# Output projections by three single-pass products, the low parts of their weights on GpSimd

## The reference

```
for l in range(DEPTH):                      # 2
    h = rmsnorm(x, norm1_g[l])
    proj = h @ w_in[l]
    ya, yb, yc, yd = ...                    # pooling, attention, convolution, spatial gating
    br = jnp.einsum('bsic,icd->bsid', br, w_branch[l])
    gates = jax.nn.sigmoid(h @ w_gate[l] + b_gate[l]).reshape(B, S, N_BRANCH, D)
    merged = jnp.sum(gates * br, axis=2)
    x = x + merged @ w_out[l]
    h2 = rmsnorm(x, norm2_g[l])
    x = x + swiglu(h2, ...)                 # l = 0, dense
    x = x + moe_ffn(h2, ...)                # l = 1, top 2 of 8 experts
```

## Time and profile before

| | us |
|---|---|
| runs shown (3) | 1772.56, 1776.92, 1777.15; median 1776.92 |
| profiled execution | 1776.46 |
| its span | 1773.4 |
| PE busy | 1642.1 (93%) |
| DVE busy | 1327.5 (75%) |
| ACT busy | 1097.2 (62%) |
| POOL busy | 323.4 (18%) |

### The profile page before, as it was taken

One profiled execution on the slowest core, in us unless ns is written; L12 is line 12 of the kernel. 1 busy time (PEld: TensorE's weight loads), 2 busy tenths in 40 slices (PEclk: granted clock), 3 DMA queues, 4 the chain that ended last, 5 costly groups with the idle time before them and its releaser, 6 DMA issues.

```text
span 1773.4 us, 22987 instructions
## 1 busy us (share of the span) xinstructions
PE 1642.1 (93%) x9076; PEld 1411.0 (80%) x9076; DVE 1327.5 (75%) x1346; ACT 1097.2 (62%) x1236; POOL 323.4 (18%) x93
## 2 busy tenths in 40 slices
PE   2987998999897789779999999999999999999998
PEld 2977976999797788468888878878888888888786
DVE  2779454545467955368988998988898888989896
ACT  3572614333456362257777877877877877777775
POOL 6758530000365854020000000000000000000000
PEclk9988999999999899889999999999999999999999
DMA  7533435555544233869999999999999999999991
GB/s 184 178 121 104 132 119 181 180 186 190 179 131 143 87 127 119 296 237 363 354 368 340 360 352 334 375 348 341 375 345 349 366 341 352 365 341 355 364 362 44
DMA packets 231254, 460.55 MB, mean 260 GB/s; under 512 B 7418, under 2 KB 79334, under 8 KB 231142
## 3 DMA queue, kind: packets, MB, share of 16 engines
q1 hardware_dynamic: 229888, 456.68, 73.3%
q0 software_dynamic: 832, 1.74, 0.6%
q10 hardware_dynamic: 422, 0.61, 0.1%
HBM read 457.96 MB, written 1.05 MB: 259 GB/s over the span
## 4 chain that ended last, share of the span: by engine, by line
PE 80%; DVE 15%; ACT 2%; issue 1%; DVEq 0%; ACTq 0%
PE bank L905 17%; PE bank L906 17%; PE bank L909 17%; PE bank L690 6%; PE bank L692 6%; PE bank L691 6%; DVE arena L1440 3%; PE bank L735 3%; PE bank L933 2%; PE bank L940 2%; PE bank L969 1%; DVE shared8k L1583 1%; DVE shared8k L1455 1%; DVE qk_raw L1373 1%; ACT w_hi L496 1%
## 5 line engine op out<-in xcount | busy, mean ns | idle before, releaser
L547 DVE TENSOR_TENSOR w_lo<-arena,w_hi 128x1024 fp32r<-128x1024 f32 x486 | 579.2, 1220 | 81.4 <-ACT w_hi L541 69.5
L541 ACT ACTIVATE w_hi<-arena 128x1024 fp32r<-128x1024 f32 x492 | 517.4, 1061 | 146.9 <-PE bank L909 146.6
L504 POOL TENSOR_TENSOR w_lo<-ring,w_hi 128x2048 fp32r<-128x2048 f32 x56 | 293.9, 5254 | 377.5 <-ACT w_hi L496 377.5
L905 PE MATMUL bank<-w_hi,h_hi 128*128 128x512 f32 x896 | 358.5, 400 | 1.4 <-DVE h_lo L1657 1.4
L906 PE MATMUL bank<-w_hi,h_lo 128*128 128x512 f32 x896 | 349.1, 390 | 0.0
L690 PE MATMUL bank<-h_hi,w_hi 128*128 128x256 f32 x992 | 292.1, 294 | 27.3 <-POOL w_lo L504 22.1
L691 PE MATMUL bank<-h_lo,w_hi 128*128 128x256 f32 x992 | 288.0, 290 | 0.0
L692 PE MATMUL bank<-h_hi,w_lo 128*128 128x256 f32 x992 | 287.6, 290 | 0.0
L909 PE MATMUL bank<-w_lo,h_hi 128*128 128x512 f32 x896 | 276.4, 390 | 0.0
L547 DVE TENSOR_TENSOR w_lo<-ring,w_hi 128x1024 fp32r<-128x1024 f32 x180 | 215.0, 1220 | 27.0 <-ACT w_hi L541 23.0
L541 ACT ACTIVATE w_hi<-ring 128x1024 fp32r<-128x1024 f32 x180 | 189.8, 1062 | 54.3 <-PE bank L909 54.2
(11 more groups left out here) (235 smaller groups left out, 1920.3 us busy)
## 6 DMA issues: line engine op xcount, KB each, us to landing
arena<-in_moe_w SPq DMA_DIRECT2D x246, 1024.0 KB, 5.8
ring<-in_moe_w SPq DMA_DIRECT2D x90, 1024.0 KB, 5.8
ring<-in_ffn_w SPq DMA_DIRECT2D x33, 1024.0 KB, 5.3
ring<-in_w_gate SPq DMA_DIRECT2D x32, 1024.0 KB, 5.3
ring<-in_w_in SPq DMA_DIRECT2D x16, 1024.0 KB, 5.3
ring<-in_w_branch SPq DMA_DIRECT2D x8, 1024.0 KB, 4.8
ring<-in_w_out SPq DMA_DIRECT2D x8, 1024.0 KB, 4.8
x_tok<-in_x SPq DMA_DIRECT2D x2, 512.0 KB, 6.2
```

The source lines that it names most:

```text
L504: eng.tensor_tensor(w_lo[:, m % LO, :], raw, w_hi[:, m % HI, :].bitcast(F32), ALU.subtract)\
L541: nc.scalar.activation(half_hi[:, m % AHEAD, :], raw_of(n)[:, HALF * (m % 2):HALF * (m % 2) + HALF], ACT.Copy)\
L547: eng.tensor_tensor(half_lo[:, m % AHEAD, :], raw_of(m // 2)[:, HALF * (m % 2):HALF * (m % 2) + HALF], half_hi[:, m % AHEAD, :].bitcast(F3 ...
L905: pe.matmul(dst, hi, w[:, cols], start=first(x), stop=False)
```

## The change

The output projections leave the fp32 form. Each of their products is made by `three`, from high and low parts of `merged` and of the weights. Four things follow. The "out" units are in the list of splits, so ACT makes their high parts and GpSimd, behind the last branch unit, their low parts. `merged` is split too: DVE raises `merged_summed` in place of `merged_ready`, ACT copies two slices at a time into `h_hi` and raises `merged_hi`, and DVE subtracts into `h_lo` and raises `merged_ready`; DVE's subtraction for q comes after its sum for q + 1. ACT splits o0 and o1 ahead of its four copies and o2 and o3 behind them. And an "out" unit frees its slot of the ring when its low part is made.

```diff
@@ class Plan, unit
-        if key[0] != "out":
-            self.split[n] = len(self.splits)
-            self.splits.append(n)
+        self.split[n] = len(self.splits)
+        self.splits.append(n)
...
@@ lo_engine
-            if kind in ("in", "gate", "branch"):
+            if kind in ("in", "gate", "branch", "out"):
                 return "pool"
             return "dve"
...
@@ TensorE, acc_unit
-                if ukey[0] == "out":
-                    w = wait_raw(pe, plan.index[ukey]).rearrange("p (k d) -> p k d", k=2)
-                else:
-                    w, wl = parts(pe, ukey, "p (k d) -> p k d", 2)
+                w, wl = parts(pe, ukey, "p (k d) -> p k d", 2)
...
-                            if ukey[0] == "out":
-                                last = pe.matmul(bank[b][:, :], lhs(k, t), w[:, k, cols], start=start, stop=stop)
-                            else:
-                                last = three(bank[b][:, :], lhs(k, t), (w[:, k, cols], wl[:, k, cols]), start, stop)
+                            last = three(bank[b][:, :], lhs(k, t), (w[:, k, cols], wl[:, k, cols]), start, stop)
...
-                    acc_unit(("out", l, u), ("out", l), lambda k, t: merged[:, 2 * u + k, P * t:P * t + P], u == 0, u == 3)
+                    acc_unit(("out", l, u), ("out", l), 
+                             lambda k, t: (h_hi[:, 2 * u + k, P * t:P * t + P], h_lo[:, 2 * u + k, P * t:P * t + P]), u == 0, u == 3)
...
@@ ScalarE, after the last y_hi
+                hi_until(plan.split[plan.index[("out", l, 1)]])
+                for q in range(4):
+                    act_e.wait_ge(merged_summed, 4 * l + q + 1)
+                    fn(h_hi[:, 2 * q:2 * q + 2, :], merged[:, 2 * q:2 * q + 2, :], ACT.Copy).then_inc(merged_hi, 1)
+                hi_until(plan.split[plan.index[("out", l, 3)]])
...
@@ VectorE, the sums
                             if n == 3:
-                                ins.then_inc(merged_ready, 1)
+                                ins.then_inc(merged_summed, 1)
...
+                        if n == 3:
+                            for x in ([q - 1] if q >= 1 else []) + ([3] if q == 3 else []):
+                                dve.wait_ge(merged_hi, 4 * l + x + 1)
+                                tt(h_lo[:, 2 * x:2 * x + 2, :], merged[:, 2 * x:2 * x + 2, :], h_hi[:, 2 * x:2 * x + 2, :].bitcast(F32),
+                                   ALU.subtract).then_inc(merged_ready, 1)
```

More of the change, by code:

```diff
@@ L441, in trunk_kernel @@
         pooled_ready = sem("pooled_ready")
+        merged_summed = sem("merged_summed")
+        merged_hi = sem("merged_hi")
         merged_ready = sem("merged_ready")
```

## The result

| | before | changed |
|---|---|---|
| median of the runs (5 each) | 1773.68 us | 1787.32 us (1784.94 to 1791.62) |
| ratio | | 1.0073, 95% interval 1.0053 to 1.0093 |
| profiled execution | 1776.46 | 1785.63 |
| its span | 1773.4 | 1783.9 |
| first single-pass (before: fp32) product of the projection, layer 0 | 251.22 | 261.49 |

The page of the changed kernel: the fp32 line is gone from the chain, DVE's share grew by a point and PE's fell by two.

The account below looks back on a forecast made before the run. TensorE was taken to bound the kernel (80% of the chain, VectorE 15%). Per layer -5.85 + 2.05 + 4.3 + 3.75 + 1.75 = +6.0 us, +12.0 for two on 1776.46, giving 1788.5; range 1777 to 1794.

Parts of the forecast that it names:

- the first case: Branch products: two VectorE sums a layer stand still for GpSimd's new subtractions; 1785 to 1792 us, chance 0.70.
- First collision: Third branch product: a VectorE sum waits for GpSimd's low part of the first output unit; +4.3 us a layer.
- Second collision: Late branch products: a VectorE sum waits for GpSimd's low part of the second output unit; +3.75 us a layer.
- Splitting `merged`: Before the projection: the first product also waits for one more multiply and sum, then a subtraction; +2.05 us a layer.
- Start of the projection: Layer 0: first product starts at 261.3 instead of 251.2 us, after both waits and the split of `merged`.
- Products: Output projection: 96 single-pass products take 21.9 us in place of 27.73, saving 5.85 us a layer.
- Clock: TensorE's new idle times bring half speed that may reach into the projection; +1.75 us a layer taken, 0 to 5.1.
- o2 and o3: Projection: GpSimd's low parts of the third and fourth output units come just in time; cost 0 by 0.3 us.
- What follows moves as a block: After the projection: the chain of later steps keeps its spacing and only shifts; no added cost.
- The first rival: Both VectorE waits occur but the clock is untouched; 1785.0 us, lower end of the case with chance 0.70.
- the one-collision case: Branch products: only one VectorE wait a layer, the second unit's subtraction falling after the sums; 1777.5 to 1781 us, chance 0.14.
- the side of a gain: Branch products: VectorE keeps its port and GpSimd's subtraction waits, so no sum stands; 1768.9 us, chance 0.08.

Follow-up runs that it names:

- fillers: Changed kernel plus matmuls nobody reads, placed where TensorE stands around the third and fourth branch products in each layer; 1783.5 us, ratio 1.0043 to before.
- psum_after: Changed kernel with VectorE writing bank times gate back into the bank, so each sum has one PSUM input; 1760.9 us, ratio 0.9918 to before.
- short_lows: Changed kernel with GpSimd's subtractions for all eight output units cut to 128 of 2048 columns; 1770.4 us, ratio 0.9966 to before.
- short_o1: Changed kernel with only the GpSimd subtraction of each layer's second output unit cut to 128 of 2048 columns; 1774.9 us, ratio 0.9994 to before.
- short_o0: Changed kernel with only the GpSimd subtraction of each layer's first output unit cut to 128 of 2048 columns; 1778.4 us, ratio 1.0011 to before.
- both psum kernels: The edit that gives each sum one PSUM input, made in the changed kernel (1760.9 us, ratio 0.9918) and in the kernel before (1769.9 us, 0.9969).
- lows_on_dve: Changed kernel with the low parts of the output units made on VectorE instead of GpSimd; 1775.3 us, ratio 1.0003 to before.
- the two single cuts: Changed kernel with GpSimd's subtraction cut to 128 columns for only the first output unit (1778.4 us) or only the second (1774.9 us).

## Why the prediction was right, point by point

The measured 1787.3 lies 1.2 from the forecast of 1788.5, in the first case. Part of that closeness is luck. The forecast was +12.0 on a profiled execution of 1776.46. The change itself came out as +13.0 by the ratio (interval 9.4 to 16.5), on a median of before that was 2.8 lower, and as +9.2 from profiled execution to profiled execution.

- *First collision:* forecast +4.3, measured 4.91 - 0.69 = 4.2. Right, also in place.
- *Second collision:* forecast +3.75, measured 4.23 - 0.69 = 3.5. It struck the last quarter of the third product's sums instead of the third; in the run with fillers, where PE keeps its full clock, it struck the third, as computed for that case (251.97). For half speed inside the branch products the prediction had put it on the first sum of the last product, one sum too late. The half speed of 245.6 to 249.1 had made PE's third product and with it o1's split about 1.5 later (250.56 less 0.60, where I had 248.4).
- *Splitting `merged`:* forecast +2.05. From the end of the first sum (258.81 + 0.69) to the first product 1.99, less the 0.06 of before: 1.9.
- *Start of the projection:* forecast 261.3, measured 261.49 less 0.60 of lag, 260.9.
- *Products:* forecast 21.9. 24.22 less half of 4.6 is 21.9; and 22.05 at full clock in psum_after. The Trainium skill (FP8 and Floating Point Precision, TensorE Precision Notes) counts true fp32 as four passes, and the estimate from that, three of four, was 20.8. The row was the better guide.
- *Clock:* taken at 1.75 a layer, bounds 0 and 5.1; measured 2.2 and 2.9, and 5.3 for both by the fillers. Mis-sized by 1.5 over both layers, on the low side.
- *o2 and o3:* forecast just in time. GpSimd was done at 276.4, and no idle row stands between the 96 products in either layer. Right.
- *What follows moves as a block:* wrong. At the end of the second projection the changed trace lags 13.4 (742.32 against 728.95), at the end of the span 10.5. The place is the first expert's selection; timelines of DVE and PE, changed kernel first, then before:

```profile
771.44 2.76 DVE L1652 TENSOR_SCALAR arena<-const,place,chosen 128x128 f32<-128x128 f32 x2 [3.85 <-issue]
...
774.26 5.67 PE L929 MATMUL bank<-arena,shared8k 128*128 128x128 f32 x32 [8.37 <-DVE arena L1652]
```

```profile
758.12 4.85 DVE L1646 TENSOR_SCALAR arena<-const,place,chosen 128x128 f32<-128x128 f32 x2 [4.06 <-issue]
...
763.03 6.37 PE L933 MATMUL bank<-arena,shared8k 128*128 128x128 f32 x32 [10.67 <-DVE arena L1646]
```

DVE's pair takes 2.76 in one and 4.85 in the other, while GpSimd runs its six subtractions of 2.31 each (13.88 from 764.86 on in the changed kernel, 13.87 from 751.33 on in before). The difference, 2.1, is about one of GpSimd's; another 0.7 is in PE's 32 products (5.67 against 6.37). The traces fall into the two kinds, PE idle 10.7 (before, short_lows, short_o1) or 8.4 (changed, short_o0, both psum kernels, lows_on_dve, fillers), and the moment at which DVE arrives sorts all nine: counting GpSimd's subtractions by 2.31 each, the pair starts 0.1 to 0.15 before the end of one of them in the three slow traces, and 0.36 to 0.6 before it in the six others. It reads as if DVE needs to be there somewhat ahead of the end to get in. No run moves that moment on purpose, so this is a reading and not shown.

So 1.5 too little for the clock and 2.9 given back here work against each other, and the forecast was closer than its parts.

The first rival (no clock effect) is refuted by the 2.2 and 2.9 us that the projections take over 22.05 and by the fillers, which take them away; the one-collision case by the three long rows and by the two single cuts; the side of a gain by the order of events: GpSimd took the port inside one L1582, as it had in the trace of before.

## What to carry to other kernels

Before giving work to an idle GpSimd, list what VectorE does beside it, and by inputs: here an operation with two inputs in SBUF stood for the whole of the GpSimd instruction (4.91 beside 4.53), and one with an input in PSUM did not (0.69). If VectorE ends last there, keep one of its inputs in PSUM, or cut GpSimd's instruction short; moving the work to VectorE at half the time can be the cheaper choice (1775.3 against 1787.3). And when a wait is added ahead of TensorE, add to its price the half speed that may follow the pause, but only for the part of it that lies over work that TensorE itself ends last (5.0 us here, in two layers).

## What the runs showed of the hardware that was not expected

Idle time of TensorE was followed by half speed or not with little between the cases. Pauses of 1.54 and 1.59 us ahead of the projection drew none (psum_after, short_o1). One of 2.39 did (short_lows, 0.50 from 254.2 to 257.5), and so did 3.97 and 5.27 in the changed kernel, with stretches of 3.5 and 6.8 us at 0.50, and 4.59 in lows_on_dve. Matmuls without use in the pauses kept the clock at 1.00, and the two projections became 5.0 us shorter although these matmuls computed nothing. And beside a queue of short GpSimd instructions (2.31 each) the same pair of VectorE operations cost 2.76 or 4.85 us; the traces fit with the moment of its arrival, which no run tested.
